# A hybrid encoder step on one core: the sample's attention units, the softmax and the mLSTM loads are moved into the last head's projections

## What is computed

```python
z = rmsnorm(x) @ w_in          # -> q, k, v (attention), mq, mk, mv, mo (mLSTM), two gates
# attention: 8 query heads, 2 key heads of 64, window of 192 keys, ALiBi, a learned sink per head
p = exp(s - mx);  w = p / (sum(p) + exp(sink - mx));  att = w @ v
# mLSTM: 4 heads of 128, in blocks of frames
b = cumsum(log_f);  mt = max(b + m, max(d));  a = exp(d - mt) * (q @ k.T)
num = a @ v + exp(inter - mt) * (q @ C);  C_new = decay * C + (ws * k).T @ v
x = x + concat(att, rmsnorm_head(sigmoid(mo) * h)) @ w_out
```

## Time and profile before

| what | us |
|---|---|
| median of 3 runs | 2158.77 (2157.87 to 2160.5) |
| the profiled execution: its own time | 2161.6 |
| its span, first to last instruction | 2159.9 |
| PE busy | 2044.8 (95%) |
| VectorE, ScalarE, GpSimd busy | 1164.8, 699.6, 711.9 |
| mean DMA rate | 90 GB/s |

### The profile page before, as it was taken

The page is one execution under the profiler, slowest core; times in us unless marked ns, Lnnn a source line. Parts: engine busy times, 40 slices in busy tenths (PEclk is TensorE's granted clock), DMA queues, the critical chain, the costliest instruction groups (busy, mean ns, idle before and its releaser), DMA issues.

```text
span 2159.9 us, 38351 instructions
## 1 busy us (share of the span) xinstructions
PE 2044.8 (95%) x14285; PEld 1994.6 (92%) x14285; DVE 1164.8 (54%) x1996; ACT 699.6 (32%) x1373; POOL 711.9 (33%) x733
## 2 busy tenths in 40 slices
PE   7999999999999998999995589999999999999997
PEld 7999999999999988888884579999999999999996
DVE  6654445446666675644433443575454544566665
ACT  6333333332112235343333331333333333312112
POOL 2256555543112100321120331015555556312110
PEclk8999999999999999899997789999999999999998
DMA  7122122226222102322310642211222122622302
GB/s 244 41 91 89 60 79 70 89 80 245 100 80 80 47 27 64 114 91 76 98 63 16 183 110 75 80 58 61 80 70 89 59 89 85 238 91 80 108 13 93
DMA packets 152336, 194.82 MB, mean 90 GB/s; under 512 B 11320, under 2 KB 117848, under 8 KB 152256
## 3 DMA queue, kind: packets, MB, share of 16 engines
q1 hardware_dynamic: 144560, 174.11, 24.5%
q0 software_dynamic: 7696, 19.63, 2.9%
HBM read 142.69 MB, written 50.96 MB: 90 GB/s over the span
## 4 chain that ended last, share of the span: by engine, by line
PE 84%; DVE 5%; ACT 5%; issue 4%; DMA 1%; POOL 1%; SPq 0%; DVEq 0%; ACTq 0%; POOLq 0%
PE bank L245 26%; PE bank L247 26%; PE bank L246 26%; ACT SP L1669 2%; PE bank L2162 1%; PE bank L2152 1%; PE bank L2171 1%; DVE SP L1895 1%; PE bank L740 1%; PE bank L280 1%; DVE YO L2070 1%; DMA XIN<-in_x_prompt 1%; ACT L1669 0%; PE bank L2094 0%; DMA GU<-grow 0%
## 5 line engine op out<-in xcount | busy, mean ns | idle before, releaser
L1189 DVE SCALAR_TENSOR_TENSOR X<-bank,X 128x362 f32<-128x362 f32 (+1 forms) x528 | 275.4, 534 | 192.7 <-PE bank L247 192.7
L245 PE MATMUL bank<-HH,WGH 128*128 128x362 f32 (+2 forms) x808 | 265.4, 328 | 4.7 <-POOL HL L1550 4.7
L247 PE MATMUL bank<-HH,WGL 128*128 128x362 f32 (+2 forms) x808 | 256.9, 318 | 0.0
L246 PE MATMUL bank<-HL,WGH 128*128 128x362 f32 (+2 forms) x808 | 256.8, 318 | 0.0
L245 PE MATMUL bank<-FC,WR 128*128 128x272 f32 x768 | 223.6, 291 | 2.7 <-ACT X L690 2.4
L247 PE MATMUL bank<-FC,WR 128*128 128x272 f32 x768 | 222.6, 290 | 0.0
L246 PE MATMUL bank<-FC,WR 128*128 128x272 f32 x768 | 221.8, 289 | 0.0
L586 DVE TENSOR_TENSOR PV<-bank,PV 128x272 f32<-128x272 f32 x280 | 121.9, 439 | 147.4 <-PE bank L247 107.2
L653 POOL TENSOR_TENSOR SA<-SA,PV 128x272 f32<-128x272 f32 x160 | 136.7, 875 | 112.2 <-DVE PV L586 109.1
L245 PEld LDWEIGHTS bank<-HH,WGH 128*128 128x128 f32 x808 | 154.6, 191 | 12.6 <-issue 10.3
L245 PE MATMUL bank<-ABe,WBe 128*128 128x362 f32 (+1 forms) x480 | 158.3, 330 | 0.0
(11 more groups left out here) (349 smaller groups left out, 5594.1 us busy)
## 6 DMA issues: line engine op xcount, KB each, us to landing
asp<-SA SPq DMA_DIRECT2D x44, 544.0 KB, 3.1
AR<-asp SPq DMA_DIRECT2D x22, 1088.0 KB, 5.2
RAWG<-in_w_gate SPq DMA_DIRECT2D x22, 1024.0 KB, 5.9
RAWU<-in_w_up SPq DMA_DIRECT2D x22, 1024.0 KB, 5.2
RAWDe<-in_w_down SPq DMA_DIRECT2D x12, 1024.0 KB, 5.0
RAW<-in_w_in SPq DMA_DIRECT2D x22, 512.0 KB, 4.5
RAWDo<-in_w_down SPq DMA_DIRECT2D x10, 1024.0 KB, 5.1
xsp<-X SPq DMA_DIRECT2D x8, 1088.0 KB, 4.9
```

The source lines that it names most:

```text
L245: nc.tensor.matmul(bank[:, 0:w], w_hi, rhs_hi, start=first, stop=False)
L246: nc.tensor.matmul(bank[:, 0:w], w_hi, rhs_lo, start=False, stop=False)
L247: return nc.tensor.matmul(bank[:, 0:w], w_lo, rhs_hi, start=False, stop=last)
L1189: nc.vector.scalar_tensor_tensor(out=x, in0=BANK[DOWN_BANK[i % 6]][:, 0:w], scalar=0.5, in1=x, op0=ALU.mult, op1=ALU.add).then_inc(s_.xadd, 1)
```

## The change

* **Attention in the heads.** In PE's list the values of unit u move behind the first chain of the next unit, and the transposes behind the third chain. On ACT the exponentials of u move ahead of the eviction of the unit's first chain. On DVE the rounding of the next weights (`unit_low`) and the copy to `ATT` move into the next unit, between the softmax's first part and its normalisation (so the softmax stands in three pieces around them: `att_softmax`, `att_normalise`, `att_weights`).
* **The last head** has its 12 chains shared among six attention units, two chains each: its own four and the sample's two. The values of the last one stand inside the mLSTM's block 0.
* **The transpose of the sample's key cache** moves to the end of the first unit, and its loads, and the loads of the sample's state, ahead of the heads in POOL's list.
* **mLSTM loads**: `ZQ` of blocks 0 and 1, the first gate rows and the first `ZO` are loaded while the last head runs. The rows are two tiles, `GUU` and `GUW`, with two DMAs where there was one of the same total size. For that the tiles have other places: `ZQ` and `ZO` in the region of `RAW4`.
* **`w_out`**: its first four units are no longer loaded under the last head but behind the loads of block 2, when `ATT` has been used, into `RAWO`, which lies where `ATT` lies.
* **`HH<-ATT` and `HL<-ATT`** are made in three parts (`att_high`, `att_low`), the first under the last chains, the last one inside block 0.
* **Gates**: the Exps of blocks 0 to 2 stay behind chain 14, those of blocks 3 to 8 move behind chain 16.

The core of the diff:

```diff
...
+        ZO = place("ZO", [P, LH, P], F32, rRAW + 12288)
+        GUU = [place("GUU0", [P, LH, P], F32, rRAW + 14336), place("GUU1", [P, LH, P], F32, rT)]
+        GUW = [place(f"GUW{i}", [P, LH, P], F32, rT + 2048 * (i + 1)) for i in range(2)]
+        VM = place("VM", [P, 2, LH, LD + 2], F32, rT + 6144)
...
+        QWI = place("QWI", [P, LH, P], F32, rC + 1536)
+        RAWO = place("RAWO", [P, 4, KT, P], F32, rA)
...
-        VK_AFTER, GATE_1, GATE_2, SCAN = 14, 9, 14, (11, 12, 13)
+        VK_AFTER, GATE_1, GATE_2, SCAN = 14, 9, (14, 16), (11, 12, 13)
...
-            for t in range(4):
-                sp.wait_ge(z.lo, UNITS - 3 + t)
-                load(t, w_out, t * P)
...
-                if b >= 2:
-                    sp.wait_ge(m_.vt, b - 1)
-                    sp.wait_ge(m_.d, 2 * b - 2)
-                    wait_done(sp, m_.qw, b - 2)
                 sp.dma_start(ZQ[:, par, :, 0:L], zm[0:12, :, col:col + L].rearrange("t p c -> p t c")).then_inc(ma_in[par], 16)
-                sp.dma_start(GU[:, par, :, 0:L], rows[0:8, col:col + L].partition_broadcast(P)).then_inc(ma_in[par], 16)
+            def m_load_rows(b):
+                L, par, col = (P if b < NB else DEC), b % 2, b * P
+                sp.dma_start(GUU[par][:, :, 0:L], grow[0, :, col:col + L].partition_broadcast(P)).then_inc(gu_in[par], 16)
+                if b:
+                    sp.dma_start(GUW[par][:, :, 0:L], grow[1, :, col:col + L].partition_broadcast(P)).then_inc(gu_in[par], 16)
+            def m_load_next(b):
+                sp.wait_ge(m_.vt, b - 1)
+                sp.wait_ge(m_.d, 2 * b - 2)
+                wait_done(sp, m_.qw, b - 2)
+                m_load(b)
+                m_load_rows(b)
...
+            sp.wait_ge(z.lo, UNITS)
+            sp.wait_ge(g.out, 16 * 4)
+            m_load_rows(0)
+            sp.wait_ge(zst[0], 16 * (3 + 9 + 1))
+            sp.wait_ge(zst[3], 16 * (3 + 9 + 1))
+            sp.wait_ge(zst[2], 16 * (3 + 9 + 2))
+            m_load(0)
+            m_load(1)
             for q in range(4):
-                sp.wait_ge(zst[q], 16 * (3 + 12))
-            sp.wait_ge(t_.ev, 2 * NB + 2)
-            sp.wait_ge(att_lo, 1)
-            sp.wait_ge(g.out, 16 * 4)
-            m_load(0)
-            m_load_gate(0)
-            m_load(1)
-            for b in range(1, NB + 1):
+                sp.wait_ge(zst[(q + 1) % 4], 16 * (3 + 12))
+                if q == 0:
+                    m_load_gate(0)
+            m_load_rows(1)
+            m_load_gate(1)
+            m_load_next(2)
+            sp.wait_ge(att_lo, 3)
+            for t in range(4):
+                load(t, w_out, t * P, RAWO)
+            for b in range(2, NB + 1):
                 m_load_gate(b)
                 if b < NB:
-                    m_load(b + 1)
...
+                load(t, w_out, (4 + t) * P, RAWO)
...
+            sp.wait_ge(m_.num, NB + 1)
+            sp.wait_ge(m_.qw, NB)
+            sp.wait_ge(m_.d, 2 * NB + 2)
...
+            nc.gpsimd.memset(VM[:, :, :, LD:LD + 1], 1.0).then_inc(m_.one, 1)
+            pool.wait_ge(g.col, 1)
+            pool.dma_start(CNS[:, :, 0:LD], a["state_C"][0, 0].rearrange("h d e -> d h e")).then_inc(m_.cs, 16)
+            pool.dma_start(CNS[:, :, LD], a["state_n"][0, 0].rearrange("h d -> d h")).then_inc(m_.cs, 16)
+            pool.wait_ge(g.out, 16 * 4)
+            pool.dma_start(CKV[:, :], flat(a["cache_k"][0, 0])).then_inc(vk.cin, 16)
...
-            for t in range(2):
-                stores(LH - 1, t)
+            for i in range(5):
+                store(LH - 1, i)
             pool.wait_ge(t_.ev, 4 * (LH - 1) + 2)
...
+            pool.wait_ge(vk.cev, 1)
...
-            pool.dma_start(CKV[:, :], flat(a["cache_k"][0, 0])).then_inc(vk.cin, 16)
-            for t in range(2, 4):
...
-            pool.wait_ge(vk.cev, 1)
...
-            pool.wait_ge(att_lo, 1)
-            nc.gpsimd.memset(VM[:, :, :, LD:LD + 1], 1.0).then_inc(m_.one, 1)
-            pool.dma_start(CNS[:, :, 0:LD], a["state_C"][0, 0].rearrange("h d e -> d h e")).then_inc(m_.cs, 16)
-            pool.dma_start(CNS[:, :, LD], a["state_n"][0, 0].rearrange("h d -> d h")).then_inc(m_.cs, 16)
+            for i in range(5, 12):
+                store(LH - 1, i)
+            pool.wait_ge(t_.bias, 2 * NB + 2)
...
-                if c == GATE_2:
-                    act.wait_ge(g.u, 1)
-                    nc.scalar.activation(R2[:, :], R4[:, :], ACT.Exp, scale=-1.0)
-                    for b in range(NB + 1):
+                if c in GATE_2:
+                    if c == GATE_2[0]:
+                        act.wait_ge(g.u, 1)
+                        nc.scalar.activation(R2[:, :], R4[:, :], ACT.Exp, scale=-1.0)
+                    for b in range(3) if c == GATE_2[0] else range(3, NB + 1):
                         s0, s1 = b * P, min(b * P + P, T)
                         before = GATE[:, 1:2] if b == 0 else GATE[:, 2:3] if b == NB else R4[:, s0 - 1:s0]
-                        nc.scalar.activation(R5[:, s0:s1], R3[:, s0:s1], ACT.Exp, bias=before).then_inc(g.w, 1)
+                        nc.scalar.activation(R5[:, s0:s1], R3[:, s0:s1], ACT.Exp, bias=before)
                         nc.scalar.activation(R6[:, s0:s1], R1[:, s0:s1], ACT.Exp, bias=R3[:, s1 - 1:s1]).then_inc(g.ws, 1)
...
-            def one_head(h, last=False):
+            def evict(h, i):
+                t, w = i // 3, NTILE[i % 3][1]
...
+                nc.scalar.activation(ZST[:, i % 4, 0:w], BANK[i % 2][:, 0:w], ACT.Sigmoid if t == 3 else ACT.Copy,
...
+            def one_head(h, first=False):
                 for t in range(4):
...
-                        if n == 0:
-                            att_exps(h * 4 + t)
-                        if n == 1:
-                            att_pt(h * 4 + t)
-                    if last:
-                        continue
-                    act.wait_ge(z.mm, h * 12 + (C1 + 3 * t + 3))
+                    att_exps(h * 4 + t)
+                    evict(h, 3 * t)
+                    evict(h, 3 * t + 1)
+                    evict(h, 3 * t + 2)
                     act.wait_ge(zin[t], h * 16 + (16 + 16 * loads_until(12 + t)))
                     nc.scalar.activation(WGH[:, t], RAW4[:, t], ACT.Copy).then_inc(z.hi, 1)
-            one_head(0)
+                    att_pt(h * 4 + t)
+                    if first and t == 1:
+                        act.wait_ge(vk.ctr, 1)
+                        nc.scalar.activation(CKT[:, :], BANK[7][:, 0:P], ACT.Copy).then_inc(vk.cev, 1)
+            def att_high(n):
+                t0, w = NTILE[n]
+                act.wait_ge(z.mm, C1 + 48 - 2 + n)
+                nc.scalar.activation(HH[:, 0:4, t0:t0 + w], ATT[:, :, t0:t0 + w], ACT.Copy).then_inc(att_hi, 1)
+            one_head(0, first=True)
             with act.Fori(1, LH - 1) as h:
                 one_head(h)
-            one_head(LH - 1, last=True)
-            act.wait_ge(vk.ctr, 1)
-            nc.scalar.activation(CKT[:, :], BANK[7][:, 0:P], ACT.Copy).then_inc(vk.cev, 1)
-            for u in (2 * NB, 2 * NB + 1):
-                att_exps(u)
-                att_pt(u)
-            act.wait_ge(t_.ev, 2 * NB + 2)
-            act.wait_ge(z.mm, C1 + 48)
-            nc.scalar.activation(HH[:, 0:4, :], ATT[:, :, :], ACT.Copy).then_inc(att_hi, 1)
+            for k in range(6):
+                att_exps(4 * (LH - 1) + k)
+                evict(LH - 1, 2 * k)
+                if k == 5:
+                    att_high(0)
+                evict(LH - 1, 2 * k + 1)
+                att_pt(4 * (LH - 1) + k)
+            att_high(1)
...
             m_first(0)
+            act.wait_ge(t_.ev, 2 * NB + 2)
+            att_high(2)
             m_first(1)
-            unit_high(act, 0, loads_until(UNITS + 1))
+            unit_high(act, 0, loads_until(UNITS + 1), raw=RAWO)
...
-            def one_head(h, first=False, last=False):
+            def one_head(h, first=False):
                 for t in range(4):
                     u = h * 4 + t
                     if first and t == 0:
                         dve.wait_ge(vk.out, 16 * 6)
                     att_softmax(u, t % 2, DT0 if first and t < 2 else DT)
+                    if t:
+                        unit_low(dve, h * 4 + (11 + t), t - 1)
+                    elif not first:
+                        unit_low(dve, h * 4 + 11, 3)
+                    if first and t == 1:
+                        dve.wait_ge(g.out, 16 * 4)
+                        dve.wait_ge(g.col, 1)
+                    if t:
+                        att_out(u - 1, (t - 1) % 2, h * (2 * P) + ((t - 1) // 2) * P)
+                    elif not first:
+                        att_out(u - 1, 1, h * (2 * P) - P)
                     att_normalise(u)
                     if first and t == 0:
                         dve.wait_ge(g.out, 16 * 4)
-                        dve.wait_ge(g.col, 1)
-                    att_out(u, t % 2, h * (2 * P) + (t // 2) * P)
-                    if not last:
```

(81 more changed lines are left out.)

117 lines of the change are left out of this document (57 added, 60 removed).

## The result

The changed kernel takes 2102.73 us (median of 4 runs, 2100.47 to 2104.08), the kernel before 2158.95 beside it: a ratio of 0.9738, with a 95% interval of 0.9721 to 0.9755. That is 56.2 us, where 60.2 were forecast; the time lies 4.1 us above the forecast and inside its range. The profiled run took 2100.47 us, its span 2098.7.

The account below looks back on a forecast made before the run. PE was taken to bound the whole, but in these stretches by the waits between its pieces. Gains 13.4 + 1.0 + 47.4 + 3.4, less 5, make 60.2 us: forecast 2098.6 us, range 2086 to 2114.

Parts of the forecast that it names:

- Gates: PE's wait for ACT at the gates: moving 12 of 18 Exps gains 3.4 us, bounds 0 and 5.
- Heads: Units 1 to 11: stalls gone, a unit takes 14.97 us (three chains of 3.93 us and three pieces), 13.4 us gained.
- Unit 0: First attention unit of the heads, with its own stall: 1.0 us gained, taken between 0 and 2.0.
- Last head: Last head and sample up to the mLSTM: 66.2 us of pieces after 113.7 before, 47.4 us gained, with 1.5 us slack.
- Rival 3: Softmax doesn't hold the pace of two chains; the last head's six units stall 2 us each: 2110.6 us, chance 0.1.
- mLSTM: mLSTM up to the first output chain: 5 us longer than 58.1 (63), bounds 6 us shorter and 14 longer.
- PE waits for `ZO` 2 in `m_first(2)`: mLSTM: `ZO` of block 2, queued behind the `w_out` loads, lands at 20 to 21 us, and PE waits for it.
- Rival 1: The mLSTM doesn't stretch, as `w_out` lands while PE waits for DVE anyway: 2093 us, chance 0.2.
- rival 2: The `w_out` loads cost fully in the mLSTM, 14 us in place of 5: 2107.6 us, chance 0.18.
- Rival 4: Granted clock falls to 1.2 GHz through the heads, making the kernel slower; all 48 chains would give 2252 us; chance 0.03.

Follow-up runs that it names:

- experiment 3: Changed kernel with the exponentials alone behind the eviction of the unit's first chain again, in all heads; 2106.05 us, ratio 0.9750.
- experiment 6: Changed kernel with the rounding of `w_out`'s four units one block later on ACT and DVE; 2102.75 us, ratio 0.9741.
- experiment 7: Changed kernel with POOL's exponents of mLSTM block 0 ahead of the last head's last two stores; 2103.81 us, ratio 0.9743.
- Experiment 12: Changed kernel with block 0's exponents ahead of the last two stores, `ZO` 2 ahead of `w_out`, `w_out` loads behind block 4's `ZO`, rounding later; 2093.78 us, ratio 0.9689.
- experiment 5: The changed kernel once more, unaltered; 2101.30 us, ratio 0.9730.
- experiment 9: The same program as experiment 4, run once more; 2109.26 us, ratio 0.9765.
- experiment 1: Changed kernel with the 18 small Exps of the gates in one piece behind chain 14 again; 2105.91 us, ratio 0.9742.
- experiment 4: Changed kernel with, in heads 0 to 2, transposes behind the second chain and exponentials behind the first eviction again; 2111.32 us, ratio 0.9760.

## Where the prediction held, and where it failed

**Gates: held.** 3.4 us worked out, 3.4 measured, 3.35 when undone.

**Heads: right in kind, 1.8 us too much.** There is no wait left, as forecast. But a unit takes 15.16 us and not 14.97. The 3.93 us of a chain came from one pair of rows of the chain of waits, and that pair doesn't show the small gaps at the changes between chains and pieces: 11 units times 0.19 are 2.1 us. Unit 0, put at 1.0 us, gave 1.4. On the causes the runs are less sharp than the sum: transposes and exponentials together are worth 6.3 to 6.7 us, the exponentials' place alone nothing while the transposes stand late, and the other 6 go, by difference, with the values and DVE's order.

**Last head: held, 1.3 us too much,** in the same way: 67.6 us where the pieces make 66.2, so 0.2 us a unit. The pace of two chains was the risk; the 1.5 us of slack in the sum were enough, since PE's list has no wait ahead of L2206 in any of the six. But they hang on the exponentials' place: behind the eviction (experiment 3) two of the six wait 0.5 us. Rival 3 falls.

**mLSTM: the step that failed.** 7.3 us longer instead of 5 (5.5 to 7.6 in the profiles in which this stage is the same), within the bounds (6 shorter, 14 longer), and the mechanism was half right. That 5 came so near is in part luck: it was chosen between the bounds, and not added up from waits. Right was that the `w_out` loads would be the cause, and that `ZO` 2 would need over 6 us to land (6.5). Wrong was the sentence "PE waits for `ZO` 2 in `m_first(2)`". It didn't wait for it at all. The wait came through the engines' lists: ACT's first unit waits for the load, DVE's low half waits for ACT, and the copies that block 2 needs stand behind that in DVE's list. In the changed kernel's list the first row is ACT's, the others are DVE's:

```profile
1150.85 1.06 ACT L1262 ACTIVATE WGH<-RAWO 128x1024 fp32r<-128x1024 f32 x1 [2.72 <-DMA RAWO<-in_w_out]
...
1151.94 2.00 DVE L1266 TENSOR_TENSOR WGL<-RAWO,WGH 128x1024 fp32r<-128x1024 f32 x1 [4.50 <-ACT WGH L1262]
1153.86 0.88 DVE L1996 COPY CN<-bank 128x129 f32<-128x129 f32 x4
1154.66 0.67 DVE L1985 COPY VM<-bank 128x512 f32<-128x512 f32 x1
```

The prediction had named ACT's wait, for what is queued behind `unit_high`, but not DVE's list behind `unit_low`, whose copies PE needs first. Experiment 6 shows both: with the rounding out of the way block 2 starts 2.2 to 3.5 us earlier, and then the wait for `ZO` 2 is there, 2.73 us long. Two causes stood one behind the other, and the prediction saw only the second. What the first is worth until the second binds is 1.2 to 1.9 us at block 5's start.

**What it missed.** In block 0, POOL's exponents stand behind its last store, which waits for the last chain's copy, so they come 1.0 us behind PE's start of the block, and their running beside `HL<-ATT` makes both longer (experiment 7). This puts block 1 at 8.3 instead of 6.7 us, though alone it costs nothing that shows behind block 2. The load of ACT's Exp table in block 0, which the prediction counted, lay inside ACT's wait for POOL; with the exponents early it comes to the front.

**The rivals.** Rival 1 (no stretch) and rival 2 (14 us) both fall for the changed kernel: 7.3 lies between. Experiment 12 shows that rival 1's case could be had by another order of loads, rounding and exponents: 55.5 us, under the 58.1 of the kernel before. Rival 4 (the clock falls through the heads) falls: 1.00 in the stretch from 1040, where PE is busy for all of 40.00 us.

## What to carry to other kernels

A large load put into a queue that also feeds a running pipeline delayed the transfer behind it here, whichever that was (PE waited 5.1 us for one block's `ZQ`, and 7.5 us for its `ZO` when that came next instead), until it stood in front of a gap in which nothing was due. When such a load is moved, follow its consumers through each engine's list: the wait showed up on PE as a wait for an unrelated copy that stood behind the rounding of the loaded weights. And when several moves were made to cover one stall, undo them singly and together, and compare the programs before reading the numbers: here the run taken for one move alone had undone two, and so the share of each is still open. A landmark, too, has its own spread, to be read from profiles of unchanged code: 0.1 us for block 1's start, 2 us for the first output chain.

## What the runs showed of the hardware that was not expected

VectorE and GpSimd held each other up where both read two tiles. GpSimd's 512-element operations took 2.58 and 2.34 us beside VectorE's `HL<-ATT`, and 1.29 and 1.04 away from it (experiment 7); VectorE's took 2.35 beside them and 1.66 away from them. The times of the rows fit turns rather than sharing: VectorE's first third ends at 1138.00 and GpSimd's operation, started at 1136.55, at 1139.13, 1.13 us behind that; VectorE's second third, started at 1138.31, ends at 1140.66, 1.53 behind that again; GpSimd's second ends at 1141.55. The Trainium skill (SBUF — State Buffer, SBUF: two separate sides) states such an exclusive lock, for a VectorE operation with two inputs in SBUF against GpSimd; the trace agrees.

PE's clock came back less than expected in the mLSTM: PE arrives there at 1.00, but the stretches from 1120 and from 1160 have a granted clock of 0.83, a mean between its two levels (1.2 and 2.4 GHz). Four transposes at the start of a block took 0.60 us with no wait ahead (1135.53) and 0.63 behind 1.23 us of it (experiment 6, 1151.81), but 1.08 and 1.09 behind 4.49 and 4.76 us of it (1143.85, 1155.48). So these waits are paid twice, once as idle time and once as slower work behind it. The spread of the first output chain is in part of this kind: from block 5's start it takes 12.2 us where that block's `ZO` transposes took 1.06 us (the changed kernel, experiments 5 and 9), and 10.9 where they took 0.60 (experiments 1 and 4). For the mLSTM the prediction had put a price on the clock only within its lower bound.
